# A Fourier mixer folded twice by the symmetry of its tables, and the mixers' products in another order

## The reference, cut to what matters

```python
def _conformer_conv(h, dw_w, dw_b, ln_g, ln_b, pw_w, pw_b):
    a, g = jnp.split(h, 2, axis=-1)
    z = a * jax.nn.sigmoid(g)
    z = lax.conv_general_dilated(z, dw_w[:, None, :], ..., feature_group_count=GROUP_WIDTH) + dw_b   # 31 taps
    zg = _layernorm(z in 4 groups of 64, ln_g, ln_b)
    return jax.nn.silu(zg) @ pw_w + pw_b

def _fourier_mix(c, w, b):
    cg = c.reshape(bsz, seq, 4, 64)
    f = jnp.fft.fft2(cg, axes=(1, 3), norm='ortho').real       # over the 1024 rows and the 64 channels
    return jnp.einsum('bsgc,gce->bsge', f, w).reshape(bsz, seq, 256) + b

def _spatial_gate(h, ln_g, ln_b, w_s, b_s):
    u, v = jnp.split(h, 2, axis=-1)
    v = _layernorm(v, ln_g, ln_b)
    sv = jnp.einsum('gts,bnsgc->bntgc', w_s, v in chunks of 128 rows) + b_s
    return u * sv

# second_block
y_a = _diff_attention(...)      # 4 heads, two softmaxes each; o = _rmsnorm(o, subln_g) over 64 channels
y = jnp.concatenate([y_a, y_b, y_c, y_d], axis=-1)
x = x + y @ w_out[l]
```

## Time and profile before

| | |
|---|---|
| median of 3 runs | 3070.09 us (3069.58 to 3070.68) |
| profiled execution | 3071.74 us, span 3070.0 us |
| PE busy | 2847.2 us (93%), 15820 products |
| DVE busy | 1534.5 us (50%) |
| ACT busy | 981.3 us (32%) |
| POOL busy | 325.8 us (11%) |

### The profile page before, as it was taken

The page is one execution under the profiler, slowest core; times in us unless marked ns, Lnnn a source line. Parts: engine busy times, 40 slices in busy tenths (PEclk is TensorE's granted clock), DMA queues, the critical chain, the costliest instruction groups (busy, mean ns, idle before and its releaser), DMA issues. The chain is left out here.

```text
span 3070.0 us, 39008 instructions
## 1 busy us (share of the span) xinstructions
PE 2847.2 (93%) x15820; PEld 2292.2 (75%) x15820; DVE 1534.5 (50%) x2444; ACT 981.3 (32%) x1850; POOL 325.8 (11%) x282
## 2 busy tenths in 40 slices
PE   6999998989896999898988889899898999999998
PEld 3798886879764897786887678666444888888887
DVE  4312556778534312657766438687112444444445
ACT  3111233555412211325544242376312211121112
POOL 0000002212420001002114300000013000000001
PEclk7999998999997999998999999899998999999999
DMA  6321122015454221221153331001100111011102
GB/s 256 100 91 41 61 84 58 15 56 189 159 209 158 72 74 49 74 74 33 42 179 117 141 110 43 15 1 39 75 25 14 41 55 55 28 55 55 55 27 89
DMA packets 108119, 238.93 MB, mean 78 GB/s; under 512 B 9554, under 2 KB 64852, under 8 KB 99520
## 3 DMA queue, kind: packets, MB, share of 16 engines
q1 hardware_dynamic: 86816, 222.07, 20.6%
q10 hardware_dynamic: 21152, 14.75, 1.5%
HBM read 193.80 MB, written 42.99 MB: 77 GB/s over the span
## 5 line engine op out<-in xcount | busy, mean ns | idle before, releaser
L901 PE MATMUL ps<-xn_hi_sb,ft_hi_sb 128*128 128x512 f32 x720 | 269.0, 374 | 10.6 <-DVE ft_lo_sb L1336 10.6
L903 PE MATMUL ps<-xn_hi_sb,ft_lo_sb 128*128 128x512 f32 x720 | 264.3, 367 | 0.0
L902 PE MATMUL ps<-xn_lo_sb,ft_hi_sb 128*128 128x512 f32 x720 | 264.2, 367 | 0.0
L2862 DVE TENSOR_TENSOR arena_sb<-arena_sb,ps 128x512 f32<-128x512 f32 x256 | 173.0, 686 | 121.4 <-PE ps L2574 118.8
L849 PE MATMUL ps<-tm_hi_sb,xn_hi_sb 128*128 128x512 f32 (+2 forms) x608 | 215.6, 355 | 0.8 <-DVE xn_lo_sb L1263 0.8
L851 PE MATMUL ps<-tm_hi_sb,xn_lo_sb 128*128 128x512 f32 (+2 forms) x608 | 213.3, 351 | 0.0
L850 PE MATMUL ps<-tm_lo_sb,xn_hi_sb 128*128 128x512 f32 (+2 forms) x608 | 212.9, 350 | 0.0
L2557 PE MATMUL ps<-xn_hi_sb,w_up_hi_sb 128*128 128x512 f32 x512 | 200.6, 392 | 9.8 <-POOL xn_lo_sb L3196 9.8
L2559 PE MATMUL ps<-xn_hi_sb,w_up_lo_sb 128*128 128x512 f32 x512 | 200.4, 391 | 0.0
L2558 PE MATMUL ps<-xn_lo_sb,w_up_hi_sb 128*128 128x512 f32 x512 | 200.4, 391 | 0.0
L2574 PE MATMUL ps<-w_down_hi_sb,h_lo_sb 128*128 128x512 f32 x480 | 187.0, 390 | 0.0
(11 more groups left out here) (398 smaller groups left out, 6266.2 us busy)
## 6 DMA issues: line engine op xcount, KB each, us to landing
arena_sb<-in_w_ft SPq DMA_DIRECT2D x44, 512.0 KB, 3.5
arena_sb<-mqk_dram SPq DMA_DIRECT2D x36, 512.0 KB, 3.4
arena_sb<-in_w_ada SPq DMA_DIRECT2D x16, 1024.0 KB, 9.1
arena_sb<-in_w_up SPq DMA_DIRECT2D x16, 1024.0 KB, 6.6
arena_sb<-in_w_down SPq DMA_DIRECT2D x16, 1024.0 KB, 4.8
arena_sb<-x_dram SPq DMA_DIRECT2D x26, 512.0 KB, 5.2
arena_sb<-in_xall SPq DMA_DIRECT2D x20, 512.0 KB, 4.7
arena_sb<-mv_dram SPq DMA_DIRECT2D x40, 256.0 KB, 3.8
```

Of the source, the lines that this page charges most:

```text
L901: pe.matmul(to, hi, xn_hi_flat[:, k, at:at + size], start=k == 0, stop=False)
L902: pe.matmul(to, hi, xn_lo_flat[:, k, at:at + size], start=False, stop=False)
L903: mm = pe.matmul(to, lo, xn_hi_flat[:, k, at:at + size], start=False, stop=k == KT - 1)
```

## The change

- The tables over the rows shrink to one, `dft_s` [128, 2, 1024]: cosines and sines for even and for odd frequencies, over the first 256 rows only. It is loaded once all scores are made; `w_out2` follows once all heads are turned.
- VectorE folds the input `c2_t` [128, 2, 1024] before the transform: row n with row 1024 - n (sum and difference, `c_sum`, `c_diff`), and then n with 512 - n (`folded`, four parts of 256). Row 256 of the sums goes into a table `turned` of alternating signs. The three parts of `fold` stand in attention's last block, behind the `combine` of heads 0, 1 and 2.
- The channel transform is applied to the folded parts: 16 products of 128 columns in place of 16 of 256. The row transform of a channel half is nine products of 255 to 257 columns in place of 24.
- The result comes in even and odd frequencies; `spectrum` writes every second element of `y_t`, forwards and backwards.
- TensorE's list is put in another order (first the means of the convolution, now ahead of the last `values`; then channel table, gate products, variances, channel transform, `head_squares`, both transforms, the first half of the pointwise product, the gate's transposes, its second half), those of ScalarE and VectorE accordingly. Banks of the four gate, channel and transform products are `SIDE` = 4, 5, 7, 6.

In the diff, of the long pieces of the mixers (from line 2435 on) the removed lines are left out ("..."); they stand in the functions printed above.

```diff
@@ -111,10 +111,13 @@
...
-    ang = 2 * np.pi * ((n[:, None] * n[None, :]) % SEQ) / SEQ
...
-    out["cos_s"] = np.cos(ang[:, 0:half + 1]).reshape(NX, P, half + 1).transpose(1, 0, 2).astype(f)
-    out["sin_s"] = np.sin(ang[:, 1:half]).reshape(NX, P, half - 1).transpose(1, 0, 2).astype(f)
+    fold = np.zeros((SEQ // 4, SEQ))
+    rest, even, odd = n[0:SEQ // 4, None], 2 * np.arange(half // 2 + 1)[None, :], 2 * np.arange(half // 2)[None, :] + 1
+    for at, table, freq in ((0, np.cos, even), (257, np.sin, even[:, 1:-1]), (512, np.cos, odd), (768, np.sin, odd)):
+        fold[:, at:at + freq.shape[1]] = table(2 * np.pi * ((rest * freq) % SEQ) / SEQ)
+    fold[0, 768:] = np.sin(np.pi * odd[0] / 2)
+    out["dft_s"] = fold.reshape(2, P, SEQ).transpose(1, 0, 2).astype(f)
...
@@ -406,10 +409,13 @@
...
-        cos_s = arena[:, XNT:XNT + KT * (HALF + 1)].rearrange("p (k n) -> p k n", k=KT)
-        sin_s = arena[:, XNT + KT * (HALF + 1):XNT + 8192].rearrange("p (k n) -> p k n", k=KT)
-        u_tm = part(M2, NX, 2, 2, P)
-        odd = [part(M2 + 6144 + 512 * j, HALF) for j in range(2)]
+        QUAR = SEQ // 4
+        dft_s = part(XNT, 2, SEQ)
+        c_sum, c_diff = part(M2 + 16448, 2, HALF), part(M2 + 17472, 2, HALF)
+        folded = part(M2, 4, 2, QUAR)
+        turned = part(YT + 6144, 2, QUAR + 1)
+        u_tm = part(M2 + 2048, 4, 2, 2, P)
+        odd = [part(M2 + 16448 + 512 * j, HALF) for j in range(2)]
...
@@ -2173,7 +2179,9 @@
...
-tab_ld = [sem(f"tab_ld{n}") for n in range(2)]
+tab_ld, c_fold = sem("tab_ld"), sem("c_fold")
+FOLD_ALL = 12
+SIDE = (4, 5, 7, 6)
...
@@ -2232,9 +2240,10 @@
...
-    sp.wait_ge(d_pv, 2 * NX)
-    sp.dma_start(cos_s, A["cos_s"]).then_inc(tab_ld[0], 16)
-    sp.dma_start(sin_s, A["sin_s"]).then_inc(tab_ld[1], 16)
+    for m in range(2):
+        sp.wait_ge(d_s[m], 4 * NX)
+    sp.dma_start(dft_s, A["dft_s"]).then_inc(tab_ld, 16)
+    sp.wait_ge(d_t, 4 * NX)
...
@@ -2435,64 +2444,52 @@
             for m in range(2):
                 scores(h, 0, 0, h, m)
         each(NX, query_block)
+        pe.wait_ge(cv_acc, 2)
+        for j in range(2):
+            pe.wait_ge(d_e[j], 4 * NX)
+            group_mean(dw_acc, j, mu_mm)
         for half in range(2):
             values(NX - 1, 1, half)
+    def group_mean(src, n, done):
+        for c in range(2):
+            mm = pe.matmul(ps[:, 2 * n + c, :], mean64, src[:, n, 512 * c:512 * (c + 1)], start=True, stop=True)
+        mm.then_inc(done, 1)
     def mixers():
...
+        pe.wait_ge(d_q, 2 * NX)
         for j in range(2):
             for m in range(2):
...
+                mm = pe.matmul(ps[:, 7, (2 * j + m) * P:(2 * j + m + 1) * P], dft_c[:, m, :], fnet_w[:, j, :], start=True, stop=True)
         mm.then_inc(cw_mm, 1)
...
+        pe.wait_ge(ln_v, 1)
+        for g in range(4):
+            if g == 0:
+                pe.wait_ge(d_t_act, 4 * NX)
+            if g == 2:
+                pe.wait_ge(cw_ev, 1)
+            if g == 3:
+                pe.wait_ge(d_y, NX)
+            v_g = uv_tm[:, :, GW + DH * g:GW + DH * (g + 1)]
+            pe.matmul(ps[:, SIDE[g], :], sgu_w[:, g, :], v_g, start=True, stop=True).then_inc(sg_mm, 1)
         for j in range(2):
             pe.wait_ge(mu_sq, j + 1)
             group_mean(z_flat, j, var_mm)
...
+        pe.wait_ge(c_fold, FOLD_ALL)
         for n in range(4):
...
+            pe.wait_ge(sg_u, n + 1)
+            for i in range(2):
+                for j in range(2):
+                    mm = pe.matmul(ps[:, SIDE[n], (2 * i + j) * P:(2 * i + j + 1) * P], folded[:, n, j, i * P:(i + 1) * P],
+                                   chan_w[:, j, n // 2, :], start=True, stop=True)
+            mm.then_inc(u_mm, 1)
         def head_squares():
             pe.wait_ge(o_square, 2)
             pe.wait_ge(o_eps, 1)
...
+            pe.wait_ge(var_ln, 2)
             for j in range(2):
                 for c in range(2):
                     pe.matmul(ps[:, 2 * j + c, :], mean64, o_sq[:, j, 512 * c:512 * (c + 1)], start=True, stop=False)
@@ -2503,17 +2500,40 @@
                                            start=False, stop=i == 3)
                 mm.then_inc(o_var, 1)
+        def dft(j):
+            a, b = SIDE[2 * j], SIDE[2 * j + 1]
+            for at, n, to in ((0, 0, ps[:, a, 0:QUAR + 1]), (QUAR + 1, 2, ps[:, a, QUAR + 1:HALF]),
+                              (HALF, 1, ps[:, b, 0:QUAR]), (HALF + QUAR, 3, ps[:, b, QUAR:HALF])):
+                width = to.shape[1]
+                for i in range(2):
+                    mm = pe.matmul(to, u_tm[:, n, i, j, :], dft_s[:, i, at:at + width], start=i == 0, stop=i == 1 and n > 0)
+                if n == 0:
+                    mm = pe.matmul(to, chan_w[:, j, 0, :], turned[:, j, :], start=False, stop=True)
+            mm.then_inc(dft_mm, 1)
+        def pointwise(c):
+            for e in range(2):
+                for k in range(2):
+                    mm = pe.matmul(ps[:, 2 * e + c, :], pw_w[:, k, e * P:(e + 1) * P], z_flat[:, k, 512 * c:512 * (c + 1)],
+                                   start=k == 0, stop=k == 1)
+                mm.then_inc(pw_mm, 1)
+        head_squares()
+        pe.wait_ge(u_ev, 4)
+        pe.wait_ge(tab_ld, 16)
         for j in range(2):
...
+            dft(j)
+        pe.wait_ge(cn_silu, 2)
+        pe.wait_ge(o_ln, 2)
+        pointwise(0)
+        for n in range(4):
+            pe.wait_ge(dft_odd, n // 2 + 1)
+            pe.wait_ge(dft_y, n // 2 + 1)
+            j, half = n // 2, n % 2
+            for i in range(4):
+                mm = pe.transpose(ps[:, SIDE[n], i * P:(i + 1) * P], uv_tm[:, 4 * half + i, j * P:(j + 1) * P], ident[:, :])
+            mm.then_inc(sg_tr, 1)
+        pointwise(1)
     def output():
         def product(t, u):
@@ -2759,11 +2779,33 @@
...
+        def fold(part):
+            if part == 0:
+                dve.wait_ge(q_mm, 2 * NX)
+                dve.wait_ge(c_ev, 2)
+                dve.tensor_tensor(c_sum[:, :, 1:], c2_t[:, :, 1:HALF], c2_t[:, :, :HALF:-1], ALU.add).then_inc(c_fold, 1)
+                dve.tensor_tensor(c_diff[:, :, 1:], c2_t[:, :, 1:HALF], c2_t[:, :, :HALF:-1], ALU.subtract).then_inc(c_fold, 1)
+            elif part == 1:
+                dve.wait_ge(c_fold, 2)
+                for n, src, op in ((0, c_sum, ALU.add), (1, c_sum, ALU.subtract), (2, c_diff, ALU.subtract), (3, c_diff, ALU.add)):
+                    dve.tensor_tensor(folded[:, n, :, 1:], src[:, :, 1:QUAR], src[:, :, :QUAR:-1], op).then_inc(c_fold, 1)
+            else:
+                for n, op in ((0, ALU.add), (1, ALU.subtract)):
+                    dve.tensor_tensor(folded[:, n, :, 0:1], c2_t[:, :, 0:1], c2_t[:, :, HALF:HALF + 1], op).then_inc(c_fold, 1)
+                dve.memset(folded[:, 2, :, 0:1], 0.0).then_inc(c_fold, 1)
+                dve.tensor_copy(folded[:, 3, :, 0:1], c_diff[:, :, QUAR:QUAR + 1]).then_inc(c_fold, 1)
+                middle = c_sum[:, :, QUAR:QUAR + 1]
+                dve.tensor_copy(turned[:, :, 0::2], middle.to_broadcast([P, 2, P + 1])).then_inc(c_fold, 1)
+                dve.tensor_scalar(turned[:, :, 1::2], middle.to_broadcast([P, 2, P]), -1.0, None, ALU.mult).then_inc(c_fold, 1)
...
+                if last and h < 3:
+                    fold(h)
...
@@ -2780,31 +2822,35 @@
         for j in range(2):
             dve.wait_ge(mu_mm, j + 1)
             dve.tensor_tensor(dw_acc[:, j], dw_acc[:, j], ps_flat[:, 1024 * j:1024 * (j + 1)], ALU.subtract).then_inc(mu_x, 1)
+        for g in range(4):
+            dve.wait_ge(sg_mm, g + 1)
+            u = uv_tm[:, :, DH * g:DH * (g + 1)]
+            dve.scalar_tensor_tensor(out=u, in0=ps[:, SIDE[g], :].rearrange("p (n c) -> p n c", n=NX), scalar=sgu_b[:, g:g + 1], in1=u,
+                                     op0=ALU.add, op1=ALU.mult).then_inc(sg_u, 1)
         for j in range(2):
             dve.wait_ge(var_rs, j + 1)
             dve.tensor_tensor(dw_acc[:, j], dw_acc[:, j], z_flat[:, j], ALU.mult).then_inc(cn_z, 1)
...
+        def spectrum(j):
+            dve.wait_ge(dft_mm, j + 1)
+            dve.wait_ge(dft_odd, j + 1)
+            even, uneven = ps[:, SIDE[2 * j], 0:QUAR + 1], ps[:, SIDE[2 * j + 1], 0:QUAR]
+            y, b = y_t[:, 4 + j, :], fnet_b[:, j:j + 1]
+            dve.tensor_scalar(y[:, 0:SEQ:HALF], even[:, 0:QUAR + 1:QUAR], b, None, ALU.add)
+            for src, add, first in ((even[:, 1:QUAR], odd[j][:, 0:QUAR - 1], 2), (uneven, odd[j][:, QUAR - 1:HALF - 1], 1)):
+                dve.scalar_tensor_tensor(out=y[:, first:HALF:2], in0=src, scalar=b, in1=add, op0=ALU.add, op1=ALU.add)
+                ins = dve.scalar_tensor_tensor(out=y[:, SEQ - first:HALF:-2], in0=src, scalar=b, in1=add, op0=ALU.add, op1=ALU.subtract)
+            ins.then_inc(dft_y, 1)
+        spectrum(0)
+        for n in range(2):
+            dve.wait_ge(o_rs, n + 1)
+            dve.scalar_tensor_tensor(out=y_t[:, n, :], in0=y_t[:, n, :], scalar=sub_g[:, :], in1=o_sq[:, n, :],
```

(79 more changed lines are left out.)

53 lines of the change are left out of this document (removed).

## The result

The changed kernel takes 3033.74 us (median of 4 runs, 3031.12 to 3034.59), the kernel before 3069.84 beside it; the ratio is 0.9881 (95% interval 0.9864 to 0.9898). The profiled execution took 3034.59 us, its span is 3032.8: 37.2 us less than before.

A forecast was written before the change was run, and what follows sets the result against it. The stretch from the last head's transposes to the first output product was taken as TensorE's, with three holes. Terms -42.4 + 5.8 - 1.8 + 1.0 = -37.4 us gave a 3032.7 median, said as 3033; range 3026 to 3042.

The forecast's parts named there:

- mixers: From the last head's transposes to the first output product: 46.3 us against 88.72, so 42.4 less.
- fold: VectorE in attention's last block: 6.2 us of operations, 0.4 covered, making the last transposes 5.8 us later.
- clock ahead of the output: First output records: hole shrinks from 3.76 to 2.0 us, full clock gives 1.8 us back.
- clock in attention's last block: Holes opened by the fold on TensorE lower the clock; first means and values lose 1 to 3 us, counted 1.
- ahead of the first mark, and behind the output's start: Before the combine of the last block's first head, and after the first output product starts: no change counted.
- Prices on TensorE: An f32 record costs 0.43 us at 512 columns, 0.215 to 0.235 at 256, 0.114 at 128.
- Rival 4: TensorE's narrow products don't shrink with their columns (weight-loading floor): 11.6 us more, 3044; 3%.
- What had to be on time: Mixers: Silu 8 us early for `pointwise`(0), second spectrum one microsecond ahead of the last transposes.
- rival 3: Spectra or head norm late, opening a hole ahead of TensorE's last transposes: 3035 to 3037; 9%.
- Rival 1: Fold hidden in attention's last block, neither 5.8 nor 1.0 paid: -44.2 us, 3026; 7%.
- rival 2: Clock low at the mixers' start and again ahead of the output: -33.6 us, 3036.5, or half, 3035; 18%.
- rival 5: Clock falls in attention's last block and stays at 1.2 GHz through the mixers: slower than before, 3077; 1%.

The follow-up runs named there:

- e9: The changed kernel executed a second time with nothing altered; 3034.92 us, one run.
- e10: The changed kernel executed a third time with nothing altered; 3029.41 us, one run.
- e4: Changed kernel with the pointwise product back in one piece ahead of the head squares, ScalarE's copies with it; median 3048.55 us.
- e1: Changed kernel with all three parts of the fold moved behind the last combine, out of attention's last block; median 3026.22 us.
- e5: Changed kernel with two idle f32 products of 512 columns in TensorE's 2.0 us hole ahead of the first output product; median 3032.46 us.
- e6: Changed kernel with POOL's first two output stages started once the first half of the pointwise product is copied; median 3029.86 us.
- e2: Kernel before with the fold's twelve VectorE operations added in attention's last block, results unused; median 3073.48 us, ratio 1.0013.

## Why the prediction was right, point by point

Said was 3033 us, from 3026 to 3042; measured were 3033.74. By its terms, against the profiled executions (sums: -37.4 said, -37.2 measured):

| term | predicted us | measured us |
|---|---|---|
| mixers | -42.4 | -42.53 |
| fold | +5.8 | +4.91 |
| clock ahead of the output | -1.8 | 0 (after, e9), -1.7 (e10) |
| clock in attention's last block | +1.0 | 0 |
| ahead of the first mark, and behind the output's start | 0 | +0.65, -0.23 |

- **Prices on TensorE.** Half the columns cost half: 32 records of 128 columns in 3.57 us (3.65 said), the transforms in 7.88 (7.8). Rival 4, a floor under narrow products, is out.
- **What had to be on time.** Silu, on ScalarE,

```profile
2165.43 2.37 ACT L3155 ACTIVATE arena_sb<-arena_sb,small_sb 128x1024 f32<-128x1024 f32 x2
```

ended 26.0 us after the last transposes began, said was near 27; `pointwise`(0) asked at 35.4. The second spectrum ended at 39.0 (2180.27 and 0.48), as said, and the last transposes had to wait for nothing. The thin slack held, so rival 3 did not occur; e4 shows what stood behind it. Every second element, forwards or backwards, costs nothing beside the length: the operations of 255 and 256 start 0.39 to 0.40 us apart, where 0.40 was said and 1.6 more per spectrum was the upper bound. The rule quoted there (the Trainium skill, Advanced Engine Details and Errata, "SBUF Cachelines") agrees with this.
- **The fold** was serial, as argued from the closed round. The size was 0.9 too high, 0.7 of it because the third part was priced at 1.3 us and took 0.62: the two operations of 256 and 258 elements start 0.2 apart and were priced at 0.4 each like those that read two operands, and the four small ones take 0.22 together and not 0.5. The 0.4 for VectorE's wait was right (0.38). The sign that was to show it, the last `turn_p` 5 to 7 us later, came out at 5.56, but only 4.91 of that is the fold. Rival 1 is out for the place where the fold stood, and e1 shows that 5 us later in the same list it is free. The prediction asked only whether the place chosen gave cover, not whether another one did.
- **The clock** was the part that was right by luck. The 1.8 back at the output was counted as certain, and came in neither the first nor the second execution of the changed kernel. (The prediction's signs also said that the output products take as long as before, which does not go with its own 1.8; they did.) The 1.0 in the last block was priced on the first means and values behind the last transposes, and there the clock was at 1.00. It fell earlier in the block (0.55 and 0.59 from 2130 to 2134), and that cost nothing. The same two windows in e9, the same kernel:

```profile
2130.00:2132.00 2.00, 2.00 (x22) 1.35 (x19) 2.00 (x4) 0.59 (x1) 0.00 (x0) 1.00 0.00 0
2132.00:2134.00 2.00, 0.82 (x8) 0.58 (x6) 2.00 (x4) 0.11 (x1) 0.00 (x0) 1.00 0.02 4
```

  The block is 19.07 us with the fall (after, e4, e10) and without it (e5, e9). VectorE is busy for all of both windows in either execution: it sets the pace there, and the slower products end before it asks for them. So the 1.8 that did not come stands against 1.0 and 0.9 (the fold) that were not paid, and the other terms (0.1 in the mixers, 0.4 outside them) leave a difference of 0.2 in the sum. The rule weighed there (the Trainium skill, TensorE: Matmul & The Clock Gate, Part 4, transposes count differently as busy time) would have made it 3 in place of 1. No run here separates transposes from the holes between them, and those of the earlier trace rows stand behind a hole of 2.14 us, so the rule itself is neither borne out nor refuted; the price of 3 was wrong, as nothing was paid.
- Rivals 2 and 5 did not occur as told. Of rival 2 only the half at the output came: the clock fell there and nothing came back, while the start of the mixers ran at full clock. In the changed kernel the clock was low for about 4 us at a time here, far from the 75 of rival 5.

## What to carry to other kernels

An addition to a closed round (each step waits for the one before, over several engines) costs nearly its full length, here 4.91 of 5.29 us, and the same work some microseconds further on in the same engine's list can cost nothing: look for the engine's longest idle time between the inputs' arrival and the result's first reader. When an order is changed, it has to be changed on every engine that hands work over; TensorE's order alone gave 6.2 of 12.8 us, because VectorE's list still had the slow step first. In this case a hole cost its length and the low clock behind it where TensorE was the one waited for afterwards (the output), and nothing where VectorE was (the last block); reading which columns the first consumer needs (POOL's stage, e6) removed one.

## What the runs showed of the hardware

- A hole of 2.0 us behind dense products (44 us of them in after) let the granted clock fall to 0.5 in three of seven executions, for 1.7 us of loss; one of 3.8 us did so in both executions looked at (before, e2).
- Half the columns cost half the time down to 128 columns: an f32 record took 0.43 us at 512, 0.22 at about 256 (36 in 7.88 us) and 0.11 at 128 (32 in 3.57 us).
- Writing every second f32 element, forwards or backwards, cost VectorE no more than the 0.40 us to which dense writing comes by the earlier trace rows: operations of 255 and 256 elements started 0.39 to 0.40 us apart.
- After a hole of 8.29 us the same 16 records took 9.61 us in one execution and 8.82 in another, so the loss behind a hole varies by 0.8 us.
- The time of an unchanged part, up to the first mark, varied by 4.3 us between executions (2120.1 to 2124.4), more than several of the terms above. Differences between marks came out again to 0.05 us.
